# A two-block transformer pass on one core: the order of weight strips at eight stage borders, and which engine scales the mixed heads

## The reference

```python
# first block
h = rmsnorm(x, norm_mix);  proj = h @ w_in
ya = mla(...); yb = fox(...); yc = chunk_rel(...)     # widths 512, 256, 256
y = concatenate([rmsnorm(ya, ga), rmsnorm(yb, gb), rmsnorm(yc, gc)])
x = x + y @ w_o
x = x + softmax(q k^T) v @ w_co      # q = rmsnorm(x) @ w_cq, k and v from mem (256 rows)
gate, up = split(rmsnorm(x, norm_ffn) @ w_gu)
x = x + (silu(gate) * up) @ w_down
x = rmsnorm(x, final_norm)
# second block, layer 0: pool mixer
h = modulate(rmsnorm(x), shift, scale);  u, z = split(h @ w_in)
p = causal_multiscale_pool(u)
y = einsum('bsgc,gcd->bsgd', p, w_group) * scale
x = x + gate * ((y * silu(z)) @ w_out)
# layer 1: sliding-window attention, keys and values shared over heads
k, v = modulate(rmsnorm(x), shift, scale) @ w_kv
q, z = split(modulate(rmsnorm(x), ...) @ w_in)
x = x + gate * ((attention(q, k, v) * silu(z)) @ w_out)
return rmsnorm(x, final_g)
```

## Time and profile before

| | |
|---|---|
| three runs | 2589.64, 2590.39, 2582.77 us, median 2589.64 |
| profiled execution | 2588.47 us, span 2586.7 us, mean granted clock 0.982 |
| PE busy | 2475.3 us (96%) |
| DVE / POOL / ACT busy | 1282.4 (50%) / 1136.5 (44%) / 599.2 us (23%) |
| DMA | 170.97 MB, mean 66 GB/s |

### The profile page before, as it was taken

One profiled execution on the slowest core, in us unless ns is written; L12 is line 12 of the kernel. 1 busy time (PEld: TensorE's weight loads), 2 busy tenths in 40 slices (PEclk: granted clock), 3 DMA queues, 4 the chain that ended last, 5 costly groups with the idle time before them and its releaser, 6 DMA issues.

```text
span 2586.7 us, 30782 instructions
## 1 busy us (share of the span) xinstructions
PE 2475.3 (96%) x12078; PEld 2050.2 (79%) x12086; DVE 1282.4 (50%) x1528; ACT 599.2 (23%) x1189; POOL 1136.5 (44%) x519
## 2 busy tenths in 40 slices
PE   6999999999899999999999989999999999999987
PEld 5787788887777888888888868787878777888876
DVE  5337556625463444444452677352623466055565
ACT  3111545412430000000000332010110123155532
POOL 5534754034033444444444434443444443555355
PEclk9999999899999999999999989999999999999998
DMA  5511000021011323232321111111111113100033
GB/s 180 163 41 50 1 1 34 1 106 41 17 41 58 130 98 130 97 130 87 137 80 46 49 33 49 41 49 49 49 49 49 42 47 130 42 25 26 17 114 114
DMA packets 45935, 170.97 MB, mean 66 GB/s; under 512 B 4590, under 2 KB 9456, under 8 KB 40456
## 3 DMA queue, kind: packets, MB, share of 16 engines
q1 hardware_dynamic: 37832, 148.52, 16.4%
q10 hardware_dynamic: 8000, 21.01, 2.4%
HBM read 156.90 MB, written 12.57 MB: 66 GB/s over the span
## 4 chain that ended last, share of the span: by engine, by line
PE 85%; DVE 10%; ACT 2%; issue 2%; POOL 1%; DMA 0%; ACTq 0%; DVEq 0%; SPq 0%; POOLq 0%
PE ps L507 23%; PE ps L508 22%; PE ps L510 22%; PE ps L667 6%; PE ps L645 4%; PE ps L655 3%; DVE h_lo L446 2%; DVE sq_sum L350 1%; DVE h_lo L443 1%; DVE y_lo L2335 1%; PE ps L521 1%; PE ps L523 1%; PE ps L522 1%; DVE pool_b L2304 1%; DVE tmp L435 0%
## 5 line engine op out<-in xcount | busy, mean ns | idle before, releaser
L1182 POOL TENSOR_TENSOR split_hi<-raw,cf 128x1024 fp32r<-128x1024 f32 x198 | 387.3, 1956 | 1221.5 <-PE ps L510 1111.2
L507 PE MATMUL ps<-h_hi,split_hi 128*128 128x512 f32 x2072 | 830.6, 401 | 36.3 <-DVE h_lo L446 9.5
L508 PE MATMUL ps<-h_lo,split_hi 128*128 128x512 f32 x2072 | 811.4, 392 | 0.0
L510 PE MATMUL ps<-h_hi,split_lo 128*128 128x512 f32 x2072 | 663.1, 392 | 0.0
L1184 POOL TENSOR_TENSOR split_lo<-raw,split_hi 128x1024 fp32r<-128x1024 f32 x198 | 558.6, 2821 | 15.5
L507 PEld LDWEIGHTS ps<-h_hi,split_hi 128*128 128x128 f32 x2072 | 392.6, 189 | 124.9 <-DVE h_lo L446 13.2
L510 PEld LDWEIGHTS ps<-h_hi,split_lo 128*128 128x128 f32 x2072 | 391.6, 189 | 82.8
L508 PEld LDWEIGHTS ps<-h_lo,split_hi 128*128 128x128 f32 x2072 | 392.8, 190 | 76.8 <-issue 1.9
L507 PE MATMUL ps<-act_hi,split_hi 128*128 128x512 f32 x352 | 138.8, 394 | 3.9 <-DVE act_lo L2224 3.8
L508 PE MATMUL ps<-act_lo,split_hi 128*128 128x512 f32 x352 | 137.6, 391 | 0.0
L655 PE MATMUL ps<-cf,p 128*128 128x128 f32 x712 | 124.3, 280 | 11.7 <-ACT p L797 8.5
(11 more groups left out here) (320 smaller groups left out, 3588.4 us busy)
## 6 DMA issues: line engine op xcount, KB each, us to landing
raw<-in_strips SPq DMA_DIRECT2D x198, 512.0 KB, 3.4
ada_raw<-in_ada SPq DMA_DIRECT2D x32, 1024.0 KB, 5.6
xT<-in_xT SPq DMA_DIRECT2D x4, 1024.0 KB, 6.8
xT<-in_xT ACTq DMA_DIRECT2D x4, 1024.0 KB, 8.2
out_T<-out_sb SPq DMA_DIRECT2D x16, 256.0 KB, 2.2
x_spill_d<-xT ACTq DMA_DIRECT2D x1, 3584.0 KB, 12.0
xT<-x_spill_d ACTq DMA_DIRECT2D x2, 1792.0 KB, 8.3
swa_vec_d<-vbc ACTq DMA_DIRECT2D x1, 3064.0 KB, 19.4
```

Source lines behind the costliest of these rows:

```text
L507: pe.matmul(acc[:, a:b], w_hi, hi[:, a:b], start=first, stop=False)
L508: pe.matmul(acc[:, a:b], w_hi, lo[:, a:b], start=False, stop=False)
L510: mm = pe.matmul(acc[:, a:b], w_lo, hi[:, a:b], start=False, stop=last)
L1182: pool.tensor_tensor(hi, raw[:, r, :], ones[:, 0:1].to_broadcast([P, D]), ALU.mult).then_inc(hi_split, 1)
```

## The change

1. **Mixed heads.** The MLA scaling runs on ACT behind each chunk group (`after_act`); the fox scaling is one DVE tensor_tensor (L955); POOL keeps the third.
2. **W_o.** The turns use banks 4 to 7. Strips 0 and 1 are both multiplied while turning (f < 4), then strip 1's tiles 4 to 7. Results rotate over four pairs.
3. **CQ, FFN, gates, KV.** Strip 0 stops before its last tile, strip 1 runs some tiles, then strip 0's last tile, `norm_sum`, and the rest of strip 1. At CQ strip 1 runs four tiles in between, at the first FFN tile two. CQ strip 2 still writes pair 0. At the gates and at KV it runs three, `norm_sum`, its tile 3, strip 0's last, the shift columns, tile 4, `norm_spread`, the rest.
4. **CO.** Strip 0 goes by halves of the tokens; its first half waits for four of the eight cross groups only.
5. **Next strips.** The first two u strips, and BIN 0 and 1, run as 0 to 4, 0 to 3, 5 to 7, 4 to 7. The second `unscaled` copy on DVE moves into the split chain, at its tile 3.
6. **Pool outputs.** Output tiles 0 and 1 take pieces 0 and 1 each, then pieces 2 and 3 each.
7. **Last gate.** The add, four reciprocals of 128 columns and the product go to six attention steps.

The heads and W_o, the last gate among them:

```diff
-        def mixed_scale(dve, part, t):
+        def mixed_scale(act, t):
+            a, b = mix_columns[0]
+            act.wait_ge(y_inv, 1)
+            act.activation(ytok[:, t, a:b], ytok[:, t, a:b], ACT.Copy, scale=ystat[:, 2, t:t + 1]).then_inc(y_scaled, 1)
+        def mixed_scale_part(eng, part, done):
             a, b = mix_columns[part]
-            g = QT * part + t
-            dve.tensor_scalar(ytok[:, t, a:b], ytok[:, t, a:b], ystat[:, 2, g:g + 1], None, ALU.mult).then_inc(y_scaled, 1)
+            eng.wait_ge(y_inv, 2)
+            eng.tensor_tensor(ytok[:, :, a:b], ytok[:, :, a:b],
+                              ystat[:, 2, QT * part:QT * part + QT].unsqueeze(2).to_broadcast([P, QT, b - a]), ALU.mult).then_inc(done, 1)
         def mixed_act(act, g):
             mixed_square(act, g)
             if g == 2 * QT - 3:
                 mixed_root(act, 0, 1)
+            if g >= 2 * QT:
+                mixed_scale(act, g - 2 * QT)
         def mixed_dve(dve, g):
             if g == 2 * QT - 1:
                 mixed_inverse(dve, 0, 1)
-            if g >= 2 * QT:
-                mixed_scale(dve, 0, g - 2 * QT)
...
-        def last_gate(dve, half, link):
+        def last_gate(dve, half, i, link):
...
             z = swa_z[:, NK - 1, out_tokens[half]]
-            dve.wait_ge(z_exp, half + 1)
-            link(dve.tensor_scalar(z, z, 1.0, None, ALU.add))
-            link(dve.reciprocal(z, z))
-            dve.tensor_tensor(z, z, bank(2 + half), ALU.mult).then_inc(bin_z, 1)
+            if i == 0:
+                dve.wait_ge(z_exp, half + 1)
+                link(dve.tensor_scalar(z, z, 1.0, None, ALU.add))
+            elif i <= 4:
+                part = z[:, (i - 1) * P:i * P]
+                link(dve.reciprocal(part, part))
+            elif i == 5:
+                dve.tensor_tensor(z, z, bank(2 + half), ALU.mult).then_inc(bin_z, 1)
         def swa_step_dve(dve, u, link):
-            if u in (OUT_FROM - NK, OUT_FROM):
...
             def turn_mixed(f):
-                if f < 6:
-                    pe.wait_ge(y_scaled, QT if f < 4 else 2 * QT)
+                if f < 4:
+                    pe.wait_ge(y_scaled, QT)
+                elif f < 6:
+                    pe.wait_ge(y_mid, 1)
                 else:
                     pe.wait_ge(y_last, 1)
...
+                    if j == 2:
+                        reached(pe, att_mix, "normed", 3 * QT)
                     for t in range(4):
-                        mm = pe.transpose(bank(2 + j % 4, P, t * P), ytok[:, 4 * c + t, f * P:(f + 1) * P], ident)
+                        mm = pe.transpose(bank(4 + j % 4, P, t * P), ytok[:, 4 * c + t, f * P:(f + 1) * P], ident)
```

```diff
+            def wo_part(j, ks):
+                return product(pe, pair(j % 4), (S_WO + j) % 2, h_pieces(ks), start=ks[0] == 0, stop=ks[-1] == NK - 1)
+            turn_mixed(0)
+            for f in range(NK):
                 if f + 1 < NK:
                     turn_mixed(f + 1)
                 pe.wait_ge(y_lo_done, 2 * f + 2)
-            turn_mixed(0)
-            for j in range(8):
+                if f == 0:
+                    strip_split(pe, S_WO)
+                mm = wo_part(0, [f])
+                if f < 4:
+                    if f == 0:
+                        strip_split(pe, S_WO + 1)
+                    wo_part(1, [f])
+            mm.then_inc(strip_done[S_WO % 2], 1)
+            wo_part(1, range(4, NK)).then_inc(strip_done[(S_WO + 1) % 2], 1)
+            for j in range(2, 8):
...
-                product(pe, pair(j % 2), s % 2, all_h, before=mixed_tile if j == 0 else None,
-                        free=h_free if j == 7 else None).then_inc(strip_done[s % 2], 1)
...
+                product(pe, pair(j % 4), s % 2, all_h, free=h_free if j == 7 else None).then_inc(strip_done[s % 2], 1)
...
+            def strip_part(s, acc, ks, before=None, free=None):
+                return product(pe, acc, s % 2, h_pieces(ks), before=before, free=free, start=0 in ks, stop=NK - 1 in ks)
+            split_of = as_split(pe, sp_cross)
+            strip_split(pe, S_CQ)
+            pe.wait_ge(wo_res, 5)
+            strip_part(S_CQ, pair(0), range(NK - 1), before=split_of)
+            strip_split(pe, S_CQ + 1)
+            pe.wait_ge(wo_res, 6)
+            strip_part(S_CQ + 1, pair(1), range(4))
+            split_of(NK - 1)
+            strip_part(S_CQ, pair(0), [NK - 1]).then_inc(strip_done[S_CQ % 2], 1)
+            norm_sum(pe, n_cross)
+            strip_part(S_CQ + 1, pair(1), range(4, NK)).then_inc(strip_done[(S_CQ + 1) % 2], 1)
...
+                pe.wait_ge(cq_evac, j - 1)
+                product(pe, pair(j % 2), s % 2, all_h).then_inc(strip_done[s % 2], 1)
...
-                if u == 0:
-                    eng.wait_ge(cq_evac, 4)
+                if u in (0, 2):
+                    eng.wait_ge(cq_evac, 3 + u // 2)
             attention_pe(pe, att_cross, cross_ready)
-            reached(pe, att_cross, "o_mid", QT)
-            for j in range(4):
+            strip_split(pe, S_CO)
+            for half, tok in enumerate(out_tokens):
+                reached(pe, att_cross, "o_mid", (half + 1) * QT // 2)
+                for e in range(2):
+                    mm = product(pe, pair(e)[:, tok], S_CO % 2, [(4 * e + k, h_hi[:, k, tok], h_lo[:, k, tok]) for k in range(4)], HALF)
+                    if half:
+                        mm.then_inc(strip_done[S_CO % 2] if e else co_tile, 1)
```

Gates, u strips and pool outputs on PE, the fox scaling and the moved copy on DVE. FFN is written like CQ, and KV with BIN like the gates with the u strips:

```diff
-                    for e in range(2):
-                        def before(j):
-                            if e == 0:
-                                split_there(pe, sp_gates, j)
-                            if e == 0 and j == NK - 2:
-                                pe.wait_ge(ffn_res, 8 * (FFN_GROUPS + 1))
-                                norm_sum(pe, n_pool)
-                        strip_split(pe, s0 + e)
-                        product(pe, pair(e), e, all_h, before=before, free=h_free if e else None)
-                        if e:
-                            pe.wait_ge(n_pool["sem"]["root"], 1)
-                        shift_columns(pe, bank(5 - e, 2), e, 0).then_inc(strip_done[e], 1)
...
-                        if e == 0:
-                            norm_spread(pe, n_pool)
...
+                    strip_split(pe, s0)
+                    strip_part(s0, pair(0), range(NK - 1), before=as_split(pe, sp_gates))
+                    strip_split(pe, s0 + 1)
+                    strip_part(s0 + 1, pair(1), range(3), free=h_free)
+                    pe.wait_ge(ffn_res, 8 * (FFN_GROUPS + 1))
+                    norm_sum(pe, n_pool)
+                    strip_part(s0 + 1, pair(1), [3], free=h_free)
+                    split_there(pe, sp_gates)
+                    strip_part(s0, pair(0), [NK - 1])
+                    shift_columns(pe, bank(5, 2), 0, 0).then_inc(strip_done[0], 1)
+                    strip_part(s0 + 1, pair(1), [4], free=h_free)
+                    norm_spread(pe, n_pool)
+                    strip_part(s0 + 1, pair(1), range(5, NK), free=h_free)
+                    pe.wait_ge(n_pool["sem"]["root"], 1)
+                    shift_columns(pe, bank(4, 2), 1, 0).then_inc(strip_done[1], 1)
+                    strip_split(pe, s0 + 2)
+                    pe.wait_ge(unscaled_read, 1)
+                    strip_part(s0 + 2, pair(0), range(5), before=as_split(pe, sp_pool))
+                    strip_split(pe, s0 + 3)
+                    pe.wait_ge(unscaled_read, 2)
+                    strip_part(s0 + 3, pair(1), range(4))
+                    strip_part(s0 + 2, pair(0), range(5, NK), before=lambda j: split_there(pe, sp_pool, 5 + j))\
+                        .then_inc(strip_done[0], 1)
+                    strip_part(s0 + 3, pair(1), range(4, NK)).then_inc(strip_done[1], 1)
+                    pe.wait_ge(shift_read, 2)
+                    norm_sum(pe, n_end1)
...
-                    product(pe, pair(j % 2), st % 2, all_h, before=as_split(pe, sp_pool) if begin and j == 0 else None)\
-                        .then_inc(strip_done[st % 2], 1)
-                    if begin and j == 1:
-                        pe.wait_ge(shift_read, 2)
-                        norm_sum(pe, n_end1)
...
+                def out_tile(o, ks, before=None):
+                    return product(pe, pair(o % 2), o // 2 % 2, [(4 * (o % 2) + k, y_hi[:, k, :], y_lo[:, k, :]) for k in ks],
+                                   before=before, start=0 in ks, stop=3 in ks)
+                strip_split(pe, s0 + 10, i, per)
+                for o in range(2):
+                    pe.wait_ge(pool_g, 4 * i + 3 + o)
+                    out_tile(o, range(2), (lambda k: pe.wait_ge(pool_ylo, 4 * i + k + 1)) if o == 0 else None)
+                out_tile(0, range(2, 4), lambda k: pe.wait_ge(pool_ylo, 4 * i + k + 3)).then_inc(pool_tile, 1)
+                out_tile(1, range(2, 4)).then_inc(strip_done[0], 1)
...
-                    for t in range(QT):
-                        mixed_scale(dve, 1, t)
```

(6 more changed lines are left out.)

154 lines of the change are left out of this document (74 added, 80 removed).

## The result

The changed kernel took 2557.61 us in the median of four runs (2556.19 to 2559.54), the kernel before 2589.02 (2582.77 to 2590.39). The ratio is 0.9884, 95% interval 0.9866 to 0.9901: 1.2% faster. 2558 was forecast. The runs of the kernel before fall in two groups: of the 29 taken beside the experiments, 14 took 2587.87 to 2592.01 us at a mean granted clock of 0.981 to 0.983 and 13 took 2577.80 to 2582.64 at 0.984 to 0.987, with two at 2585; the profiled execution (2588.47, 0.982) is of the first group.

A forecast was written before the change was run, and what follows sets the result against it. TensorE, 85% of the chain that ended last, bounds the kernel through its waits and slow-clock stretches. Terms from chunk attention to the last gate sum to -30.4 us, from 2588.5 to 2558; range 2547 to 2573.

The forecast's parts named there:

- Chunk attention, -9.4: Chunk attention: with the scaling off VectorE, a 1.84 us wait and a 7.6 us slow stretch go, 9.4 us saved.
- W_o, -7.0: W_o: waits of 5.2 us covered, 2.7 of clock regained, start 0.9 later; 7.0 us saved, bounds 3.5 and 7.9.
- the first rival: W_o: GpSimd takes the fox scaling first, VectorE's starts after its 3.61 us, low parts 3 us later; 2561, chance 0.15.
- CQ, +1.5: CQ: TensorE idles 4.2 us for the query copy; 0.5 plus 1.7 for clock minus 0.7, so 1.5 us longer.
- CO and FFN, -3.5 and 0: CO: the h_lo wait of 1.8 us and a slow stretch go, 3.5 saved; FFN: no change, bounds -3 and +1.5.
- Gates, -2.4: Gates and u strips: low tile 4 comes 1.0 us earlier, 2.5 charged for clock; 2.4 saved, bounds -5 and 0.
- KV, +7.3: KV and BIN: the sum had waited for nothing, so the reorder only delays; 7.3 us longer, bounds +4.7 and +9.
- so I charge 2.5 for the clock: Gates and KV: TensorE reaches low tile 4 too early, about 11 us at the gates, so slow matmuls cost 2.5 us.
- Pool outputs, -8.5: Pool groups: eight waits on y_lo, 8.5 us in all, go; nothing if the second pair of banks is read too late.
- Last gate, -8.4: Last gate: 4.9 us saved in the first half by quarter pieces and 3.5 in the second, together 8.4.
- Slots, nothing: Strip slots: four tiles, 5.4 us, cover GpSimd's splits of 4.7; no cost, else up to 4.7 us a border.
- The signs: Expected profile: no W_o wait over 1 us, some 10 us of L443 waits at both split chains, KV ending 7 later.

The follow-up runs named there:

- e1: The kernel before with one edit, the eight MLA scalings of 128x512 on ScalarE behind each chunk group: 2582.0 us, ratio 0.9983.
- e2: The changed kernel, with GpSimd's scaling of the third head family waiting until VectorE's scaling of the second is done: 2554.08 us.
- e12: The changed kernel once more, unedited, to see how its sections vary between executions: 2556.81 us.
- e3: The changed kernel, with the third query strip of CQ multiplied into banks 4 and 5 in place of 0 and 1: 2550.51 us.
- e6: The changed kernel, with the first FFN tile in the old order (gate strip whole, sums, up strip whole): 2559.76 us.
- e4: The changed kernel, with the two key/value strips in the old order (early sums), query strips in the new: 2552.57 us.
- e10: The changed kernel with three edits: GpSimd's scaling behind VectorE's, third query strip in banks 4 and 5, early sums at KV: 2544.27 us.
- e13: The changed kernel, with the last gate's second half computed in one attention step again, the first half still in pieces: 2559.58 us.
- e5: The changed kernel, with VectorE's first unscaled copy one tile sooner in both split chains (gates and KV): 2559.3 us.

## Why the prediction was right, point by point

- **Chunk attention, -9.4 with W_o starting 0.9 later: -8.1.** Right in mechanism and size against this profile. e1 shows that the one edit carries it, and the clock with it. What the forecast left out is that its base, the profiled execution, was of the longer group; over all runs of the kernel before the gain may be smaller (e1).
- **W_o, -7.0: -1.8 to -4.7 by the same count (the table's row plus the 0.9).** The step that failed: "As one tensor_tensor over 2048 columns ... I take 2.5". It took 5.73, since GpSimd's went first. That was the first rival, at 0.15, with its mechanism and its 3 us; e2 measured 2.1 for it; with VectorE's first the term comes out at -6.8 by the same count. The rest of the shortfall in the first profile was clock (e12).
- **CQ, +1.5: +0.9 and +2.0.** The new wait, forecast at 4.2, was 3.66. e3 shows what it and its slow stretch cost: 5.6 to 6.7.
- **CO and FFN, -3.5 and 0: together -1.8 and -4.0.** In sum near; the wait on h_lo at CO's start is gone, e6 leaves CO alone at -3.1, and it shows FFN at +1.3, within its bounds.
- **Gates, -2.4: -4.7 to -6.3, and KV, +7.3: +3.0 to +4.6.** Two steps failed in both. The first is "so I charge 2.5 for the clock", behind low tile 4. At KV the slow stretch did come, but it fell between the two waits, ahead of that tile, where PE had time to spare: behind low tile 4 the KV border took 16.5 us, which is the 12 tiles at full speed (16.3), where before it took 18.8. The windows of the changed kernel show it, 0.74 ahead of low tile 4 and 1.00 behind it:

```profile
2139.00:2149.00 10.00, 8.41 (x26) 6.44 (x27) 9.93 (x11) 3.46 (x3) 1.19 (x1) 0.74 0.15 52
2149.00:2165.00 16.00, 16.00 (x72) 13.25 (x71) 5.86 (x5) 8.07 (x7) 4.29 (x2) 1.00 0.54 230
```

The second step is the length of the split chain, which the forecast took over from before plus 0.4: from spread to low tile 4 it took 21.6 us at both borders, where before it took 23.1, as GpSimd's split had moved out of its start. At the gates low tile 4 therefore came 2.5 us earlier in the section, not 1.0. There a second slow stretch did fall behind it in the first profile,

```profile
1516.00:1532.00 16.00, 16.00 (x64) 13.07 (x65) 8.24 (x9) 6.80 (x6) 3.12 (x2) 0.89 0.00 1
```

and the rest of the border took 18.1 us; in e2, e3, e4 and e12 it took 16.5, and the gates came out at -5.1 to -6.3. That KV's reorder delays, which the forecast had said against the change, is shown by e4: 5.4 to 7.0 us (3.8 at the least, with e10).
- **Pool outputs, -8.5: -10.7.** The waits that went were 2.12 us a group, the section 2.67 a group shorter. That the remaining 0.55 is the restart of PE behind each wait (0.50 for a first matmul in place of 0.39, and its first weights) I only argue.
- **Last gate, -8.4: -5.9.** The second half's 3.5 was right (3.1 to 3.4, e13). The first half's "-3.55 and the slow stretch -1.7, +0.3" came out at 2.5 against the profile of before and at 4.6 against e1's, whose last attention has the same code and is 2.1 longer; which of the two is typical stays open. Waits of 0.59 and 0.84 stand there in place of the 3.55: 1.4 us that the sum had at nothing.
- **Slots, nothing:** no wait on a strip's split at any changed border.
- **The signs.** Three did not come as said: W_o has a wait of 2.43, where none over 1 was expected; the waits on L443's low parts are 3.2 us in sum and not 10, with 9.1 more ahead of the first u and query strips, which e5 shows to cost nothing; and KV is 3.0 us longer, not 7.

Added up by the table's first two columns: I promised 9.8 us too much (W_o 5.2, last gate 2.5, CO and FFN 1.7, chunk attention 0.4) and 10.2 too little (KV 4.3, gates 2.3, pool 2.2, the end 0.8, CQ 0.6); with the 1.8 of a later start, the profile gained 29.0 where the sum said 30.4. The errors of ten terms cancelled: that the total came within 1 us is luck, the total is better than the working behind it. It is also a total against the longer group of runs; against the median of the shorter one, 2581.65, the changed kernel is some 24 us faster.

## What to carry to other kernels

Before moving a sum or a spread behind other work, see whether it waited at all: at the gates it had waited 5.3 us and the move paid, at KV it had waited for nothing and the same pattern cost 4 to 7 us. A wait in the profile is worth what is left when it is gone: 4.5 us ahead of a strip cost nothing (e5), 3.7 us at CQ cost 5.6 to 6.7 (e3). And take more than one profile of the kernel before: its executions differ by more than most of these parts are worth. And where VectorE and GpSimd start together, or GpSimd's split may land in a chain of VectorE, decide the order by hand.

## What the runs showed of the hardware

- One VectorE instruction (tensor_tensor, 128x2048, both inputs in SBUF) took 5.73 us beside a GpSimd one of 3.61 that had started 0.02 us before it, and 2.29 alone; GpSimd's took 3.61 in both cases. In all eight profiles in which nothing ordered the two, GpSimd's started first.
- The granted clock falls in other places in executions of one and the same kernel: 16 transposes at the same place took 3.63 or 1.97 us, and W_o differed by 2.9 us by it. A single profile can't measure an edit of under 3 us there, while sections without a slow stretch repeat to 0.1 us.
- A slow stretch that falls where TensorE waits anyway costs nothing: at KV, at a clock of 0.74 over 2139 to 2149, PE was still 1.31 us early at low tile 4, and the rest of the border took 16.5 us.
